# Two experts gathered at once by products of 256 columns, and the eight experts of a pass written out one behind the other

## The reference, cut to what matters

```python
def swiglu(h, w_gate, w_up, w_down):
    return (jax.nn.silu(h @ w_gate) * (h @ w_up)) @ w_down

def moe_swiglu(h, router_w, w_gate, w_up, w_down):
    logits = (h @ router_w).astype(f32)
    top_val, top_idx = lax.top_k(logits, TOP_K)          # TOP_K = 2 of 8
    top_w = jax.nn.softmax(top_val, axis=-1)
    gates = jnp.sum(jax.nn.one_hot(top_idx, N_EXPERTS, dtype=f32) * top_w[..., None], axis=-2)
    y = jnp.zeros_like(h)
    for e in range(N_EXPERTS):
        y = y + gates[..., e:e + 1].astype(h.dtype) * swiglu(h, w_gate[e], w_up[e], w_down[e])
    return y
```

## Time and profile before

| what | value |
|---|---|
| median of three runs | 1210.81 us |
| profiled execution, its own time | 1213.52 us |
| its span | 1211.6 us |
| PE busy | 1191.1 us (98%), 6193 instructions |
| PEld busy | 1009.4 us (83%) |
| DVE busy | 980.6 us (81%) |
| ACT busy | 836.1 us (69%) |
| DMA, mean over the span | 284 GB/s, 344.03 MB |
| stage 480 to 580 us (an expert) | PE 100%, DVE 91.7%, ACT 78.9%, DMA share 0.95 at 351 GB/s |

### The profile page before, as it was taken

The page is one execution under the profiler, slowest core; times in us unless marked ns, Lnnn a source line. Parts: engine busy times, 40 slices in busy tenths (PEclk is TensorE's granted clock), DMA queues, the critical chain, the costliest instruction groups (busy, mean ns, idle before and its releaser), DMA issues.

```text
span 1211.6 us, 18799 instructions
## 1 busy us (share of the span) xinstructions
PE 1191.1 (98%) x6193; PEld 1009.4 (83%) x6193; DVE 980.6 (81%) x1117; ACT 836.1 (69%) x1023; POOL 30.9 (3%) x43
## 2 busy tenths in 40 slices
PE   7999999999999999999999999999999999999996
PEld 7997888888998888888888888888888888888885
DVE  4866555545767899899899899989989989989995
ACT  6655544435644688778778688878877877868883
POOL 0400000000120000000000000000000000000000
PEclk9999999999999699999999999999999999999999
DMA  8945655555453499999999989989999999998950
GB/s 284 391 149 177 200 175 184 198 177 171 144 170 122 135 365 359 342 349 366 346 353 353 373 313 369 363 311 377 347 348 346 363 347 343 357 381 311 372 192 35
DMA packets 142566, 344.03 MB, mean 284 GB/s; under 512 B 6112, under 2 KB 64688, under 8 KB 142528
## 3 DMA queue, kind: packets, MB, share of 16 engines
q1 hardware_dynamic: 141952, 342.34, 78.5%
q0 software_dynamic: 352, 1.09, 0.3%
q10 hardware_dynamic: 224, 0.10, 0.1%
HBM read 342.06 MB, written 1.44 MB: 284 GB/s over the span
## 4 chain that ended last, share of the span: by engine, by line
PE 94%; DVE 3%; issue 1%; ACT 1%; DMA 1%; SPq 0%; DVEq 0%; ACTq 0%
PE psum L1125 91%; PE psum L1122 3%; DMA raw<-in_w_in 1%; DVE prob L891 1%; DVE w_lo L378 0%; DVE smax L875 0%; DVE score L871 0%; DVE nmax L876 0%; DVE x_sb L819 0%; ACT w_hi L369 0%; DVE proj L924 0%; DVE x_sb L1045 0%; ACT L668 0%; ACT proj L668 0%; ACT aT_hi L654 0%
## 5 line engine op out<-in xcount | busy, mean ns | idle before, releaser
L396 DVE TENSOR_TENSOR w_lo<-raw,w_hi 128x1024 fp32r<-128x1024 f32 x528 | 627.2, 1220 | 59.3 <-PE psum L1125 33.5
L389 ACT ACTIVATE w_hi<-raw 128x1024 fp32r<-128x1024 f32 x528 | 547.8, 1060 | 128.6 <-PE psum L1125 125.9
L1125 PE MATMUL psum<-w_hi,aT_hi 128*128 128x512 f32 (+1 forms) x1232 | 448.2, 372 | 1.3 <-ACT w_hi L369 0.7
L1125 PE MATMUL psum<-w_hi,aT_lo 128*128 128x512 f32 (+1 forms) x1232 | 440.7, 366 | 0.0
L1125 PE MATMUL psum<-w_lo,aT_hi 128*128 128x512 f32 (+1 forms) x1232 | 323.4, 366 | 0.7 <-DVE w_lo L378 0.7
L1125 PEld LDWEIGHTS psum<-w_hi,aT_hi 128*128 128x128 f32 x1232 | 234.0, 190 | 38.6 <-issue 1.6
L1125 PEld LDWEIGHTS psum<-w_hi,aT_lo 128*128 128x128 f32 x1232 | 234.3, 190 | 35.0
L1125 PEld LDWEIGHTS psum<-w_lo,aT_hi 128*128 128x128 f32 x1232 | 215.7, 190 | 39.1 <-DVE w_lo L378 1.1
L378 DVE TENSOR_TENSOR w_lo<-raw,w_hi 128x1024 fp32r<-128x1024 f32 x118 | 144.8, 1233 | 48.9 <-PE psum L1125 45.8
L369 ACT ACTIVATE w_hi<-raw 128x1024 fp32r<-128x1024 f32 x118 | 124.6, 1059 | 82.3 <-PE psum L1125 74.1
L1125 PE MATMUL psum<-w_hi,heT_hi 128*128 128x512 f32 x352 | 138.5, 394 | 0.0
(11 more groups left out here) (181 smaller groups left out, 737.4 us busy)
## 6 DMA issues: line engine op xcount, KB each, us to landing
raw<-in_exp_w_down SPq DMA_DIRECT2D x88, 1024.0 KB, 7.0
raw<-in_exp_w_gate SPq DMA_DIRECT2D x80, 1024.0 KB, 6.1
raw<-in_exp_w_up SPq DMA_DIRECT2D x80, 1024.0 KB, 6.7
raw<-in_w_in SPq DMA_DIRECT2D x17, 1024.0 KB, 5.1
raw<-in_ffn_w_gate SPq DMA_DIRECT2D x22, 512.0 KB, 3.9
raw<-in_ffn_w_up SPq DMA_DIRECT2D x22, 512.0 KB, 4.9
raw<-in_ffn_w_down SPq DMA_DIRECT2D x11, 1024.0 KB, 4.8
raw<-in_w_out SPq DMA_DIRECT2D x8, 1024.0 KB, 7.9
```

Source lines behind the costliest of these rows:

```text
L389: nc.scalar.activation(w_hi[:, q % HIGHS, :], raw_piece(slot, q % 2), ACT.Copy).then_inc(hi_made, 1)
L396: eng.tensor_tensor(w_lo[:, q % LOWS, :], raw_piece(e_slot[q // 2], q % 2), w_hi[:, q % HIGHS, :].bitcast(F32), ALU.subtract).then_inc(lo_ ...
L1125: return pe.matmul(dst, a, b, start=start, stop=stop, skip_group_check=True)
```

## The change

The loop now runs over the passes. The eight experts of a pass stand one behind the other in the program (`act_expert`, `vec_expert`, `tensor_expert`), with `r` for the pass, `e` for the expert, `v` for the pair and `j` for the place in the pair. The pick matrix is 256 columns wide and holds the slots of two experts. One gather fills four PSUM banks with the tokens of both; it stands behind piece 56 of experts 1, 3 and 5, and ahead of the loop for the first pair. Experts 2, 4 and 6 find half of their gathered tokens drained already, the other half is drained during their first pieces. `spread_out` of an expert's output stands behind piece 3 of the next expert, and behind the loop's body for expert 7; the one over zeros is gone. The ten products ahead of the ranking read activations. ACT's table load stands once per pass. `xg_lo` has a place of its own, and the gain of the last norm lies in the constants' tile.

```diff
-            for again in range(5):
-                for b in range(2):
-                    ins = mm(bank(6 + b), put[:, 0:P], oe_hi[:, 512 * b:512 * (b + 1)], True, True)
-            ins.then_inc(banks_cleared, 1)
+            for again in range(WARM):
+                mm(bank(6 + again % 2), aT_hi[:, 0, 0:P], aT_lo[:, 0:2, :].rearrange("p k t -> p (k t)"), True, True)
...
                 for part in range(2):
                     for k in range(DK):
-                        dst = psum[:, 2 + k // 4, (k % 4) * P:(k % 4 + 1) * P]
-                        for t in range(TT):
-                            tokens = xg_lo(t, k) if part else xg_hi[:, t, k * P:(k + 1) * P]
-                            first_one, last_one = part == t == k % 4 == 0, part == t == 1 and k % 4 == 3
+                        dst = psum[:, k // 2, (k % 2) * SEQ:(k % 2 + 1) * SEQ]
+                        for t in range(TT):
+                            tokens = (xg_lo if part else xg_hi)[:, t, k * P:(k + 1) * P]
+                            first_one, last_one = part == t == k % 2 == 0, part == t == k % 2 == 1
                             ins = mm(dst, tokens, pick[:, t, :], first_one, last_one)
...
-            with pe.Fori(0, n_pass * N_EXPERTS) as i:
+            def tensor_expert(r, e):
+                i, v, j = N_EXPERTS * r + e, N_PAIRS * r + e // 2, e % 2
+                mine = slice(j * P, (j + 1) * P)
                 for q in range(FFN_PIECES):
-                    if q in (0, 4):
-
-                        pe.wait_ge(g_hi, 2 * i + (q // 4 + 1))
-                        pe.wait_ge(g_lo, 2 * i + (q // 4 + 1))
+                    if j == 0 and q in (0, 4, 6):
+
+                        pe.wait_ge(g_hi, 4 * v + {0: 2, 4: 3, 6: 4}[q])
+                        pe.wait_ge(g_lo, 4 * v + {0: 2, 4: 3, 6: 4}[q])
...
-                    if q == 3:
-                        spread_out(i)
+                    if e > 0 and q == 3:
+                        spread_out(i - 1, v)
...
-                    if q == 56:
+                    if j == 1 and e < N_EXPERTS - 1 and q == 56:
 
                         pe.wait_ge(e_hid, NC * i + NC)
                         pe.wait_ge(e_lo, NC * i + NC)
-                        gather(2 * i + 4)
-            spread_out(n_pass * N_EXPERTS, final=True)
+                        gather(4 * v + 8)
+
+            with pe.Fori(0, n_pass) as r:
+                with pe.If(r > 0):
+                    pe.wait_ge(x_added, (4 * N_EXPERTS) * r + 12)
+                    gather(4 * N_PAIRS * r + 4)
+                with pe.Else():
+                    pass
+                for e in range(N_EXPERTS):
+                    tensor_expert(r, e)
+                spread_out(N_EXPERTS * r + N_EXPERTS - 1, N_PAIRS * r + N_PAIRS - 1)
```

On DVE:

```diff
-            with dve.Fori(0, n_pass * N_EXPERTS) as i:
-                low_part_e(dve, i, 0)
-                gather_low(i, 0)
-                low_part_e(dve, i, 1)
-                gather_low(i, 1)
-                rstd_low(i)
-                for q in range(2, LOWS):
+            def vec_expert(r, e):
+                i, v, j = N_EXPERTS * r + e, N_PAIRS * r + e // 2, e % 2
+                if e == 0:
+                    for b in range(2):
+                        gather_low(v, b)
+                for q in range(LOWS):
                     low_part_e(dve, i, q)
-                output_low(i)
+                if j == 0:
+                    rstd_low(v)
+                if e > 0:
+                    output_low(i - 1)
                 for q in range(FFN_PIECES):
-                    if q == 3:
-                        add_output(i)
+                    if e > 0 and q == 3:
+                        add_output(i - 1)
...
-                    if q == 48:
+                    if j == 1 and e < N_EXPERTS - 1 and q == 48:
 
                         dve.wait_ge(pick_turned, i + 1)
                         mark_slots(i + 1)
+                    if j == 1 and e < N_EXPERTS - 1 and q in (58, 60):
+                        gather_low(v + 1, (q - 58) // 2)
                     low_part_e(dve, i, q + LOWS)
+                    if j == 0 and q < 2:
+                        gather_low(v, 2 + q)
```

More of the change, by code:

```diff
@@ L267, in expert_products @@
             return [(b, 2 * (q % 4) + h, slice(512 * h, 512 * (h + 1))) for h in range(2)]
-        def xg_lo(t, k):
-            return (aT_hi, aT_lo)[t][:, k, P:2 * P]
+        gain_last = cst[:, C_DEC:C_DEC + D_MODEL]
         ident = cst[:, C_ID:C_ID + P]
@@ L719, in _, with gather_high, output_high, act_expert @@
             nc.scalar.activation(rc[4][:], rc[3][:], ACT.Exp).then_inc(e2_made, 1)
+            def gather_high(v, b):
+                act.wait_ge(gathered, 4 * v + (b + 1))
+                nc.scalar.activation(aT_hi[:, 2 * b:2 * b + 2, :], bank(b).rearrange("p (k t) -> p k t", k=2), ACT.Copy).then_inc(g_hi, 1)
             act.wait_ge(route_ready, 1)
             n_pass = act.value_load(passes_i[0:1, 0:1], min_val=1, max_val=2)
[L723 to L732 removed]
+            def output_high(o):
+                act.wait_ge(piece_used, FFN_PIECES * o + (FRONT_PIECES + FFN_PIECES))
                 for b in range(2):
                     nc.scalar.activation(oe_hi[:, 512 * b:512 * (b + 1)], bank(6 + b), ACT.Copy).then_inc(oe_hi_made, 1)
[L736 to L738 removed]
+            def act_expert(r, e):
+                i, v, j = N_EXPERTS * r + e, N_PAIRS * r + e // 2, e % 2
                 for q in range(HIGHS):
[L740 to L744, removed]
+                    if e == 0 and q == 2:
+                        for b in range(4):
+                            gather_high(v, b)
+                    if e > 0 and j == 0 and q in (2, 3):
+                        gather_high(v, q)
+                    if e > 0 and q == HIGHS - 1:
+                        output_high(i - 1)
                     high_part_e(act, i, q)
@@ L1041, in add_output @@
                 for t in range(TT):
                     for half in range(2):
-                        dve.wait_ge(spread, 4 * i + (2 * t + half + 1))
+                        dve.wait_ge(spread, 4 * o + (2 * t + half + 1))
                         xs = x_sb[:, t, 512 * half:512 * (half + 1)]
-                        dve.scalar_tensor_tensor(out=xs, in0=bank(SPREAD_BANKS[2 * t + half]), scalar=gatex[:, t, bass.ds(i, 1)], in1=xs,
+                        dve.scalar_tensor_tensor(out=xs, in0=bank(SPREAD_BANKS[2 * t + half]), scalar=gatex[:, t, bass.ds(o, 1)], in1=xs,
```

122 lines of the change are left out of this document (65 added, 57 removed).

## The result

| | before | changed |
|---|---|---|
| median of the runs | 1210.76 us (1210.6 to 1210.83, four runs) | 1190.86 us (1189.72 to 1191.86, four runs) |
| ratio | 1 | 0.9836, interval 0.9819 to 0.9853 |
| profiled execution, its own time | 1213.52 us | 1189.95 us |

A forecast was written before the change was run, and what follows sets the result against it. The prediction took PE, busy all of 100 us in an expert's stretch, as the bound; -17.5 - 1.9 - 2.5 + 0.4 = -21.5 us took the median from 1210.8 to 1189.3 us, range 1186.5 to 1195.5.

The forecast's parts named there:

- the forecast's own band: Median time if the forecast holds, 1188 to 1190.5 us around 1189.3; chance 0.60.
- the rival with a low clock: First gather: the clock does not return in it, so -2.5 us becomes +0.6, 1192.4 us; chance 0.23.
- 17.5 were forecast: Repeated gathers: eight of 3.93 us (31.4 us) become three of 4.66 us (14.0 us), -17.5 us.
- The price of a 256-column product: Gathers at full clock: 0.120 us per 256-column product, against 0.110 us for 128; bounds 0.110 and 0.227 us.
- The clock returns in the gather: First gather: its 256-column stream restores full clock at about 406, so four pieces end at 413.0, not 415.55: -2.5 us.
- One of the forecast's two grounds: Clock return: 256-column stream at kernel's start, half to full speed in 6.5 us; 512-column products behind the old gather, 4.9 us.
- (a) of the small costs: DVE at starts of experts 2, 4, 6: 0.2 to 0.4 us of margin used, cost taken as 0.
- a margin of 0.35 us: Piece 6 of experts 2, 4, 6 before the change: `w_lo` ready at 519.3, PE asks at 519.66.
- The bound of 0.7 us: If DVE misses at the starts of experts 2, 4, 6: up to 0.7 us in each of three places, 2 us.
- Code and loop end: About 27 more code packets, 0.2 us (bounds 0 and 2.7); one loop end at kernel's end, 0.2 us (0.1 to 0.5).
- The base: Median of runs taken as 2.7 us under the profiled execution, so 1210.8 - 21.5 = 1189.3 us.
- -21.5: Sum of all terms: -17.5 gathers, -1.9 spread over zeros, -2.5 first gather and clock, +0.4 loop end and code.

The follow-up runs named there:

- The moved drains: Changed kernel with all four drains of a pair's gather done by ACT and DVE in the gather, none at the second expert's start; 1189.92 us, ratio 0.9823.
- The later sets: Two later sets of the unchanged changed kernel, kernel before run beside it, on two chips: 1212.21 to 1191.13 us and 1212.03 to 1190.74 us.

## Why the prediction was right

- **The time and the trace.** The measured 1190.86 us lies between the forecast's own band (1188 to 1190.5) and that of the rival with a low clock (1191 to 1193.5). The time alone could not have told them apart; the trace did.
- **What bounds the kernel.** That an instruction taken out of PE's stream is worth its distance to the next start held: 17.9 us where 17.5 were forecast. The 0.4 us more is mostly the longer first product behind a gather, which the distance from first product to next piece leaves out.
- **The price of a 256-column product.** 0.120 us was read from the first projection and came out as 0.120. The gather made narrow again cost 3.3 us more each, against 3.2 by 64 x 0.110 less 32 x 0.120.
- **The clock returns in the gather.** Forecast for 4.9 to 6.5 us behind its start, found at 5.4, and 3.5 to 5.5 in the other profiles. The first gather itself took 7.09 us, 7.1 forecast. The narrow first gather shows that this is the width and not the moment: 12 us of narrow products, all but 1.7 us of them of 128 columns, did not bring it back. The rival of the low clock is out. One of the forecast's two grounds was weaker than it looked: "half speed" at the kernel's start was read from product distances of 0.213 us alone, while the profile's own clock column shows 1.00 there (12 to 18 us).
- **The step that failed** is (a) of the small costs, the `w_lo` of piece 6 in experts 2, 4 and 6: "I take 0". The sum of DVE's work was right (7.0 to 7.2 us forecast, 7.2 found). But that is 0.4 us more than before, against a margin of 0.35 us, which is the same in the later passages of before too (616.68 + 1.22 against 618.25, for one). The forecast's own range of 0.2 to 0.4 us reached over that margin, and it still took nothing. The `w_lo` came 608.1 - 597.04 = 11.06 us behind the first piece and PE wanted it at 10.93. The bound of 0.7 us held; the value was 0.3 us a place, 1.0 in all. The moved drains, which took these waits away, show that this was the cause.
- **Code and loop end.** 27 packets forecast, 26 found; 0.2 us taken, nothing found. Written out alone, the loops change nothing that shows (0.9982 to 1.0003).
- **The base.** The forecast took the same 2.7 us for profile over median before and after. But the spread ahead of the experts is not the same from one execution to the next: the clock's fall, which it let stand at 392, moves by several microseconds within one kernel. Of the 1.6 us between 1189.3 and 1190.86, the parts that belong to the change leave 0.6 (they add up to -20.9, the rest of +0.3 among them, in place of -21.5). I take the other 1.0 for scatter of this base. The later sets, with 21.1 and 21.3 us won, speak for it, but no run shows it. That the total came this close is in part luck: +1.0 for piece 6 stood against 0.4 more from the gathers.

## What to carry to other kernels

Where PE is the bound and each product loads its own weights, look for two narrow products that share a stationary tile: 128 columns cost 0.110 us here and 256 cost 0.120, so joining them is worth nearly the whole second one. When a stream of narrow products stands where the clock is low, widen it first; it pays twice here, in the products saved and in the clock that came back. And when an engine beside the bound gets a few tenths of a microsecond more work ahead of a deadline, subtract them from the margin at that deadline: where the range of the estimate reaches the margin, put a cost on it, whatever the engine's mean load says.

## What the runs showed of the hardware

- PE busy without a gap was not enough for the full clock. At half clock, 10.6 us of products of 128 columns, each with its own weight load, did not bring it back (401.0 to 411.6, first gather narrow). Products of 256 columns did, 3.5 to 5.5 us behind the gather's start in nine profiles, and products of 512 columns 4.8 to 5.3 us behind the first piece in three.
- Once, behind such products (7 us of 128 columns, 0.9 us of one) in a stream without a gap, the clock fell from full to half (at 985.4). The falls at 401.0 and 401.2 inside narrow first gathers say less, since it fell at 399.1 and 401.7 inside wide ones as well.
- At full clock a product with its own weight load cost 0.110 us at 128 columns, 0.120 at 256 and 0.227 at 512; at half clock 0.214 at 128 and 0.213 at 256.
- A loop body of some 465 products was not fetched again at the jump back (24 packets in all), and the seven jumps cost 0.02 us together.
- The moment of the fall is not the program's. One kernel had it at 392.7, at 392.2 with a return between, and at 396.7. The low time added up to 10.2, 6.8 and 3.4 us, and the stretch to the first piece was 18.9, 18.4 and 17.2 us long.
- Ten idle products of 512 columns ahead of the ranking did not hold the clock reliably: it fell before them (391.5, 390.8), during them (392.7, 392.2) or after them (396.7).
- At a DMA share of 0.99 and 369 GB/s, with DVE busy 94.7% of the time, PE was still fed without a wait.
